# Two orders of block products changed, and a head's preparation moved on VectorE, in a two-block model kernel

## What is computed

```python
# first block
h = rms_norm(x, g_pre_mix) * (1 + scale1) + shift1
proj = h @ w_in                       # convolution, retention
x = x + gate1 * rms_norm(mix @ w_out, g_post_mix)
h = rms_norm(x, g_pre_mlp) * (1 + scale2) + shift2
f = square(relu(h @ w_fc1)) @ w_fc2   # w_fc1: 1024 x 4096
x = x + gate2 * rms_norm(f, g_post_mlp)
# second block, layer 0: pooling; layer 1: HGRN2 with 16 heads of 128
u = h @ hgrn_w_in                     # 1024 x 8192: q, forget f, values i, gate
log_f = ...; k = (1 - lb) * sigmoid(-fz)
o, S = chunk_scan(q, k, i, cumsum(log_f))   # per head
y = (rms(o) * norm_g * silu(gate)) @ hgrn_w_out
out = rms_norm(x + y, final_g)
```

## Time and profile before

| | |
|---|---|
| median of 3 runs | 1405.04 us (1405.03 to 1406.05) |
| profiled execution, its own time | 1406.52 us |
| its span, first to last instruction | 1404.7 us |
| TensorE busy | 1391.2 us, 99% |
| VectorE busy | 982.2 us, 70% |
| ScalarE busy | 647.8 us, 46% |
| mean granted clock of TensorE | 0.998 of 2.4 GHz |
| the 84 products | about 284.7 to 408.5 us |
| the 14 block products | 920 to 997.4 us |

### The profile page before, as it was taken

One profiled execution on the slowest core, in us unless ns is written; L12 is line 12 of the kernel. 1 busy time (PEld: TensorE's weight loads), 2 busy tenths in 40 slices (PEclk: granted clock), 3 DMA queues, 4 the chain that ended last, 5 costly groups with the idle time before them and its releaser, 6 DMA issues.

```text
span 1404.7 us, 22088 instructions
## 1 busy us (share of the span) xinstructions
PE 1391.2 (99%) x8666; PEld 1191.2 (85%) x8666; DVE 982.2 (70%) x1922; ACT 647.8 (46%) x1268; POOL 0.2 (0%) x4
## 2 busy tenths in 40 slices
PE   8999999999999999999999999999999999999998
PEld 7888888999998888888888888988888888888886
DVE  7887776799853335655476535499798889888645
ACT  6423345567762324542342323574345555556441
POOL 0000000000000000000000000000000000000000
PEclk9999999999999999999999999999999999999999
DMA  9647442344332224132232234213322222221221
GB/s 352 227 165 255 152 156 69 103 164 152 109 117 95 101 91 161 34 105 90 93 118 75 91 106 149 76 40 112 119 91 75 76 76 78 75 76 61 76 75 60
DMA packets 43734, 158.00 MB, mean 112 GB/s; under 512 B 4848, under 2 KB 5232, under 8 KB 43632
## 3 DMA queue, kind: packets, MB, share of 16 engines
q1 hardware_dynamic: 43344, 156.39, 32.7%
q10 hardware_dynamic: 288, 0.21, 0.0%
HBM read 154.48 MB, written 2.10 MB: 111 GB/s over the span
## 4 chain that ended last, share of the span: by engine, by line
PE 92%; DVE 4%; DMA 1%; issue 1%; ACT 1%; SPq 0%; DVEq 0%; ACTq 0%
PE PS L649 25%; PE PS L651 24%; PE PS L650 24%; PE PS L990 3%; PE PS L992 3%; PE PS L991 3%; PE PS L1046 1%; PE PS L1049 1%; PE PS L1048 1%; PE PS L1147 1%; DMA RAW<-in_ada 1%; PE PS L1151 1%; PE PS L1139 1%; PE PS L645 1%; PE PS L1079 1%
## 5 line engine op out<-in xcount | busy, mean ns | idle before, releaser
L649 PE MATMUL PS<-HH,WH 128*128 128x512 f32 (+1 forms) x880 | 337.5, 384 | 0.2 <-DVE WL L1371 0.2
L651 PE MATMUL PS<-HH,WL 128*128 128x512 f32 (+1 forms) x880 | 332.8, 378 | 0.0
L650 PE MATMUL PS<-HL,WH 128*128 128x512 f32 (+1 forms) x880 | 332.4, 378 | 0.0
L2375 ACT ACTIVATE WH<-RAW 128x1024 fp32r<-128x1024 f32 x176 | 185.3, 1056 | 134.4 <-PE PS L651 86.4
L1371 DVE TENSOR_TENSOR WL<-RAW,WH 128x1024 fp32r<-128x1024 f32 x176 | 213.8, 1219 | 19.1 <-ACT WH L2375 18.7
L649 PEld LDWEIGHTS PS<-HH,WH 128*128 128x128 f32 x880 | 165.6, 188 | 31.6 <-DVE WL L1371 1.0
L651 PEld LDWEIGHTS PS<-HH,WL 128*128 128x128 f32 x880 | 165.6, 188 | 31.3
L650 PEld LDWEIGHTS PS<-HL,WH 128*128 128x128 f32 x880 | 165.7, 188 | 29.2
L649 PE MATMUL PS<-WH,ZH 128*128 128x512 f32 x400 | 155.9, 390 | 0.0
L651 PE MATMUL PS<-WH,ZL 128*128 128x512 f32 x400 | 155.6, 389 | 0.0
L650 PE MATMUL PS<-WL,ZH 128*128 128x512 f32 x400 | 155.6, 389 | 0.0
(11 more groups left out here) (351 smaller groups left out, 2624.5 us busy)
## 6 DMA issues: line engine op xcount, KB each, us to landing
RAW<-in_w_fc SPq DMA_DIRECT2D x64, 512.0 KB, 3.4
RAW<-in_hgrn_in SPq DMA_DIRECT2D x56, 512.0 KB, 3.3
RAW<-in_pool_in SPq DMA_DIRECT2D x40, 512.0 KB, 3.4
RAW<-in_ada SPq DMA_DIRECT2D x36, 512.0 KB, 4.6
RAW<-in_w_in SPq DMA_DIRECT2D x26, 512.0 KB, 5.4
RAW<-in_pool_out SPq DMA_DIRECT2D x16, 512.0 KB, 3.3
RAW<-in_hgrn_out SPq DMA_DIRECT2D x16, 512.0 KB, 3.3
Z<-in_ada SPq DMA_DIRECT2D x12, 512.0 KB, 4.2
```

Source lines behind the costliest of these rows:

```text
L649: e.matmul(out, wh, xh, start=first, stop=False)
L650: e.matmul(out, wh, xl, start=False, stop=False)
L651: return e.matmul(out, wl, xh, start=False, stop=last)
L2375: e.activation(place(s)[0], raw(i), ACT.Copy).then_inc(whi.sem, whi(s))
```

## The change

Three edits. In `product_list` (5, g) and (4, g) change places. In VectorE's loop over the block products the steps of `prepare(0)` are taken once for each n over 10 instead of twice for each n over 3; what is left of the 14 steps is run by `run(first_head)` after the loop, as before. In ScalarE's loop a product's copy stands ahead of the high tile instead of behind it, `query(0)` and `scan_gate(0)` behind the second high tile, and `forget(1)` one turn later.

```diff
@@ product_list
-        out += [(6, g), (2, g), (4, g), (5, g)]
+        out += [(6, g), (2, g), (5, g), (4, g)]
@@ vector_program
                     scan_gate(0)
-                if n > 3:
-                    next(first_head, None)
                 block_low(2 * n + 4)
-                if n > 3:
+                if n > 10:
                     next(first_head, None)
             block_taken(*BLOCKS[-1][0:2])
             run(first_head)
@@ scalar_program
             for n in range(len(BLOCKS) // 2):
+                if n:
+                    block_copied(*BLOCKS[2 * n - 2][0:2])
                 block_high(2 * n + 3)
                 if n == 0:
                     forget(0)
-                else:
-                    block_copied(*BLOCKS[2 * n - 2][0:2])
+                block_high(2 * n + 4)
                 if n == 1:
                     query(0)
                     scan_gate(0)
-                block_high(2 * n + 4)
-                if n == 2:
+                if n == 3:
                     forget(1)
```

## The result

The changed kernel takes 1413.03 us (median of 4 runs, 1412.24 to 1414.01) against 1405.40 us for the kernel before (4 runs): ratio 1.0054, interval 1.0041 to 1.0066. It is slower by 7.6 us. The forecast was 1411.9 us, range 1409.3 to 1413.8, on the median of 1405.04 us that the kernel before had then: 6.9 us slower. The profiled execution took 1412.24 us, span 1410.4 us, mean granted clock 0.997.

The account below looks back on a forecast made before the run. TensorE, busy 99% of the span, was taken to bound the kernel. Products +0.1, ScalarE's order -0.4, late preparation +5.9, refill +0.1 and clock +1.2 gave +6.9 us on 1405.04: 1411.9 us, range 1409.3 to 1413.8.

Parts of the forecast that it names:

- Part 1: (5, g) before (4, g) among the 84 products: waits mostly move, about +0.1 us, bounds -1.0 and +0.5.
- Part 2: ScalarE's order in the block products: TensorE's hole at 942 shrinks, then VectorE is late; gain 0.4 us.
- Part 3: Head 0's late preparation on VectorE: TensorE's small_levels(0) waits, its second half (L1084) 5.9 us late.
- the 0.1 us of refill: TensorE's pipeline refill after the wait at small_levels(0), added to the sum as +0.1 us.
- The second wait: TensorE's L1084, second half of small_levels(0), waiting for VectorE's L2108: near 1 us.
- Rival C: VectorE's lateness reaches head 1 and small_levels(1) waits too: +0.5 to +2, about 1413.2 us; chance 0.1.
- the cover that the prediction gave: At head 1, VectorE's L2108 ends 1.3 us before TensorE's L1084 wants it, just covering VectorE's 0.7 us lateness.
- Rival A: TensorE's clock holds through the hole at small_levels(0), so no 1.2 us clock loss: 1410.7 us; chance 0.2.
- Rival B: The product reorder pays in full, -1.0 us, and ScalarE's order could give 1.1: 1410.1 us; chance 0.07.
- D: Faster: VectorE's late steps hidden at small_levels(0) and three TensorE holes close, gain 3.1 us, 1401.9 us; chance 0.04.
- E: The stall at small_levels(0) is only partly there: under 2.8 us, around 1406.5 us; chance 0.04.
- The clock: One half-clock stretch on TensorE after the hole at small_levels(0): 1.2 us lost, bounds 0 and 2.0.

Follow-up runs that it names:

- 24 fills: Changed kernel with 24 filler matmuls, later overwritten, ahead of TensorE's wait in small_levels(0): 1411.33 us, 1.0042 against the kernel before.
- ten steps: Changed kernel with one step of prepare(0) for each n over 3 instead of over 10, four left behind the loop: 1406.35 us, 1.0008.
- the filled kernels: Changed kernel with 28, then 24 filler matmuls ahead of TensorE's wait in small_levels(0): 1411.46 and 1411.33 us.
- the last version above: Kernel before with both orders changed, VectorE's preparation unchanged, and the next late steps on ScalarE and VectorE moved too: 1402.79 us, 0.9980.
- 28 fills: Changed kernel with 28 filler matmuls of 128 columns ahead of TensorE's wait in small_levels(0): 1411.46 us, 1.0044 against the kernel before.

## Why the prediction was right

**Part 1**, the products: +0.1 taken, +0.12 in the profiled pair, and nothing to be told by the runs. The steps were right one by one: with the 1.55 us by which this profile is ahead added, VectorE's addition for (5, 0) starts at 295.80 (294.25 + 1.55; 295.80 given) and that for (4, 0) at 297.34 (295.79 + 1.55; 297.34 given), the relu comes 1.5 us later against TensorE, the copy as the new releaser of (6, 1). (6, 1) lost 1.01 (1.05 given), (5, 1) 0.33 (0.3), and (3, 11) gained 0.34 (0.35).

**Part 2**, ScalarE's order: 0.4 taken, 0.35 in the pair, too little for the runs of this order alone to show. The low half of VectorE was the next to be late, as given.

**Part 3**, the chain behind the last weight half: 7.23 us given for L2108, 7.20 measured (1002.62 - 995.42); 5.88 for L2098, 5.86 measured. The delay at L1084 is 5.91 us, 5.9 given; the 0.1 us of refill that the sum adds to it is not seen (L1084 to the next matmul is 0.38 us with 24 fills, 0.40 before). The second wait is 0.4 us and not near 1, because the first part, at half clock, ran 0.87 us and took some of it; with ten steps, at full clock, it ran 0.55 us and the second wait is 0.70. That head 3's preparation could stand for head 0's was the choice on which this rests, and it held. The preparation alone gave the whole loss, and ten steps show that it grows with what stands behind the weight half.

**Rival C**, a second wait at head 1, did not come in the changed kernel: L2108 ends at 1016.16 there and TensorE's L1084 stands at 1018.01, with no wait. But the cover that the prediction gave was not there. It had VectorE 0.7 us later against TensorE, with its first memset at 1004.07. By its own rows that is too early: L2108 starts at 1004.00, and the memset started 0.47 us after it (1002.68 - 1002.21). Measured, VectorE is 0.94 us later: from L1084 to the end of head 1's L2108 it is 13.48 us instead of 12.54. That leaves 1.37 - 0.94 = 0.4 us of slack, and not the 1.3 of before. The slow stretch, 1.42 us on TensorE's side, made 1.85 of it. The kernel with 24 fills, without a slow stretch, has 0.48 us (1017.18 - 1016.70). With `small_levels(0)` 8.2 us later and no hole at head 0, TensorE waits at just this place.

**Rival A**, the clock holds, is what the filled kernels made: 1411.4 us, not the 1410.7 given. With 24 fills it is 6.1 us above the kernel before, where the account by places has 5.7; the 0.4 us were not traced. The argument against it was weaker than it looked: the changed kernel has the same wait of 2.04 us before 18.00 and no fall behind it. Rival B was wrong by the timelines of the first group, and by products alone (+0.5 us instead of about -1); D and E by the 4.9 us of wait.

**The clock was mis-sized.** I took 1.2 us with bounds 0 and 2.0, from the one slow stretch of the kernel before, of which part was to fall into the hole. That stretch lasts 3.4 us (18.8 to 22.2). The one behind the hole lasts 6.8, twice as long, and what it costs depends on how much of it lies in the hole: 1.4, 1.9 and 2.4 us in three profiles, and 2.4 between medians. So the upper bound was too low, and that 1.2 came near the 1.4 of the first profile is luck: half of the longer stretch lay in the hole there. With 2.4 the sum is 6.9 - 1.2 + 2.4 = 8.1 us, between the 7.6 and the 8.5 that the two comparisons gave; 8.5 is just inside the 8.7 of the range. The Trainium skill (TensorE: Matmul & The Clock Gate, Part 1) has half clock as the default that activity releases; the fall at 997 to 1000 us agrees with it, and the filled kernels, at 1.00 through the same wait, do too.

**Open.** What sets the moment of the fall was not tested. Between the two profiles of the changed kernel the later fall makes 1.1 us (16.40 - 15.33 from one L1084 to the next), and the start of the kernel another 0.8 us (283.94 - 283.18 at the first of the 84 products); how the two share the 0.7 us between the medians (1413.03 and 1413.77) was not told apart.

## What to carry to other kernels

A step taken out of an engine's gaps and put behind its last fixed task costs its own length, less the slack there, if another engine waits for its result; the hole costs clock behind its end too, here 1.4 to 2.4 us on 5.9. Before a hole in the bounding engine's order is moved, list who is late next: here the two reorderings handed most of their waits on (0.1 us lost and 0.35 us gained of 3.2), and 2.5 us were gained when the next ones late were moved as well.

## What the hardware showed

**The start of the kernel has a slow stretch that comes and goes.** Window from 14 to 24 us: kernel before, changed kernel, and the last version above:

```profile
14.00:24.00 10.00, 7.90 (x37) 6.56 (x38) 9.97 (x16) 6.90 (x14) 0.00 (x0) 0.83 1.03 409
```

```profile
14.00:24.00 10.00, 7.30 (x41) 6.07 (x42) 9.96 (x16) 6.91 (x13) 0.00 (x0) 1.00 1.03 409
```

```profile
14.00:24.00 10.00, 8.99 (x38) 7.52 (x38) 9.96 (x17) 6.90 (x13) 0.00 (x0) 0.66 1.03 411
```

The instructions are the same and the clock is not: it is low for 3.4 us, not at all, and for 6.8 us (14.6 to 21.4). In all 13 profiles this window has one of the three clocks. The changed kernel is ahead of the kernel before by 1.68 us at 22.27 us and gives part of it back in a wait that the slower one does not have; 0.8 us are left:

```profile
22.07 0.47 PE L649 MATMUL PS<-WH,HH 128*128 128x512 f32 x1 [0.65 <-DVE HL L1582]
```

The rest of the 1.55 us is no clock. In the profile of the kernel before, ScalarE gets two weight tiles of `w_in` late, and TensorE loses 0.2 us at 104 and 0.5 us at 110 us:

```profile
110.33 0.50 PE L649 MATMUL PS<-HH,WH 128*128 128x512 f32 x1 [0.23 <-DVE WL L1371]
```

A profile of one execution each would have given the change 5.7 us; it needs the account by places, or the medians.

**The clock was low for the same 6.8 us behind the hole, but from different moments on.** TensorE's last matmul before the hole started at 996.10, 996.84 and 997.00 us in three profiles, and the clock fell at 999.2, 1002.1 and 1001.1 us. The later it fell, the more of the slow stretch came behind the hole and cost time. And a float32 matmul of 128 columns of TensorE stands in the trace as two of 0.114 us each (6.41 us for 56, from 28 instructions), so that 28 fills were twice as long as I had meant.
